# Hybrid mLSTM, dilated attention and MoE block: landing places of the first adaLN weights, the order of the expert matmuls, router and output by halves

## The reference, cut to what matters

```python
mod = silu(c) @ ada_w + ada_b                      # adaLN: 1024 -> 6 * 1024 (sh_a, sc_a, gt_a, sh_f, sc_f, gt_f)
u = rms_norm(x) * (1 + sc_a) + sh_a
proj = u @ w_in                                    # mLSTM q, k, v, o, gates; attention q, k, v; branch gates
y = sigmoid(g_m) * (h_m @ w_branch_m) + sigmoid(g_a) * (h_a @ w_branch_a)
x = x + gt_a * (y @ w_out)
u = rms_norm(x) * (1 + sc_f) + sh_f
scores = sigmoid(u @ router_w)                     # 16 experts, the best group of 4, the best 2 in it
x = x + gt_f * sum_e combine_e * ((silu(u @ w_gate_e) * (u @ w_up_e)) @ w_down_e)
out = rms_norm(x) * final_norm_g
```

## Time and profile before

| | |
|---|---|
| median of 3 runs | 637.62 us (637.15 to 639.16) |
| the profiled execution's own time | 639.07 us |
| its span | 637.3 us |
| PE busy | 593.4 us (93%), 3581 matmul instructions |
| DVE busy | 326.7 us (51%) |
| ACT busy | 225.2 us (35%) |
| DMA | 184.78 MB, mean 290 GB/s over the span |

### The profile page before, as it was taken

How to read it: one execution, slowest core, us unless ns; L and a number is a source line. 1 busy time by engine, 2 the same in 40 slices (tenths; PEclk the granted TensorE clock), 3 DMA queues, 4 the chain that set the end, 5 groups by cost and what they waited for, 6 DMA issues and landing times.

```text
span 637.3 us, 8441 instructions
## 1 busy us (share of the span) xinstructions
PE 593.4 (93%) x3581; PEld 444.7 (70%) x3581; DVE 326.7 (51%) x515; ACT 225.2 (35%) x300; POOL 5.6 (1%) x13
## 2 busy tenths in 40 slices
PE   4697999999999999999999999889999999998783
PEld 4697988999998888999999886533543533533231
DVE  3895986775758977787454655302212112120103
ACT  3424658544454365665552443201111111110103
POOL 3000000000000000000000000000000000000000
PEclk9997999999999999999999997799999999999997
DMA  8996454877767867725699699199999999999981
GB/s 314 358 359 229 143 194 133 283 259 242 255 216 264 319 214 261 258 77 195 198 338 344 219 374 388 48 398 387 401 387 402 386 401 387 401 387 401 387 325 67
DMA packets 86313, 184.78 MB, mean 290 GB/s; under 512 B 5401, under 2 KB 5505, under 8 KB 86273
## 3 DMA queue, kind: packets, MB, share of 16 engines
q1 hardware_dynamic: 83746, 184.06, 79.9%
q10 hardware_dynamic: 2528, 0.16, 0.3%
HBM read 183.16 MB, written 1.05 MB: 289 GB/s over the span
## 4 chain that ended last, share of the span: by engine, by line
PE 85%; DMA 8%; DVE 3%; ACT 1%; issue 1%; SPq 1%; DVEq 0%; ACTq 0%
PE ps L1287 32%; PE ps L1295 15%; PE ps L1495 14%; PE ps L1506 7%; DMA ring<-in_w_down_e_dram 3%; PE ps L1485 2%; DMA ring<-in_w_gate_e_dram 2%; DMA ring<-in_w_up_e_dram 2%; PE ps L1529 2%; DMA raw<-in_ada_w_dram 1%; PE ps L1235 1%; PE ps L1358 1%; PE ps L1382 1%; PE ps L1397 1%; PE ps L1244 1%
## 5 line engine op out<-in xcount | busy, mean ns | idle before, releaser
L1287 PE MATMUL ps<-u_hi,hi 128*128 128x256 f32 x448 | 130.8, 292 | 9.3 <-DVE u_lo L815 9.3
L755 DVE TENSOR_TENSOR lo<-raw,hi 128x2048 fp32r<-128x2048 f32 x52 | 118.7, 2289 | 35.6 <-ACT hi L514 35.3
L1287 PE MATMUL ps<-u_lo,hi 128*128 128x256 f32 x448 | 128.7, 287 | 0.0
L1287 PE MATMUL ps<-u_hi,lo 128*128 128x256 f32 x448 | 128.6, 287 | 0.0
L1495 PE MATMUL ps<-ring,xe_t 128*64 128x512 f32 x512 | 113.8, 594 | 7.9 <-DMA ring<-in_w_up_e_dram 4.4
L514 ACT CAST hi<-raw 128x2048 fp32r<-128x2048 f32 x52 | 98.8, 1907 | 50.0 <-PE ps L1287 24.8
L1287 PEld LDWEIGHTS ps<-u_hi,hi 128*128 128x128 f32 x448 | 88.0, 196 | 9.6 <-DVE u_lo L815 9.5
L1495 PEld LDWEIGHTS ps<-ring,xe_t 128*64 128x64 f32 x512 | 37.1, 137 | 76.0 <-issue 75.7
L1287 PEld LDWEIGHTS ps<-u_lo,hi 128*128 128x128 f32 x448 | 88.0, 197 | 0.1
L1287 PEld LDWEIGHTS ps<-u_hi,lo 128*128 128x128 f32 x448 | 87.9, 196 | 0.0
L1506 PE MATMUL ps<-ring,he_t 128*64 128x512 f32 x256 | 57.1, 596 | 1.5 <-DMA ring<-in_w_down_e_dram 0.8
(11 more groups left out here) (276 smaller groups left out, 797.0 us busy)
## 6 DMA issues: line engine op xcount, KB each, us to landing
raw<-in_w_in_dram SPq DMA_DIRECT2D x42, 1024.0 KB, 5.3
ring<-in_w_gate_e_dram SPq DMA_DIRECT2D x32, 1024.0 KB, 14.6
ring<-in_w_up_e_dram SPq DMA_DIRECT2D x32, 1024.0 KB, 14.2
ring<-in_w_down_e_dram SPq DMA_DIRECT2D x32, 1024.0 KB, 14.6
raw<-in_ada_w_dram SPq DMA_DIRECT2D x24, 1024.0 KB, 5.5
raw<-in_w_branch_m_dram SPq DMA_DIRECT2D x4, 1024.0 KB, 5.5
raw<-in_w_out_dram SPq DMA_DIRECT2D x4, 1024.0 KB, 7.5
raw<-in_w_branch_a_dram SPq DMA_DIRECT2D x2, 1024.0 KB, 6.4
```

The costliest lines, as they stand in the source:

```text
L755: V.tensor_tensor(lo[b % RING][:], src[:], hi[b % RING][:].bitcast(F32), ALU.subtract).then_inc(lo_ready, 1)
L1287: ins = mm(dst, w[:, k, cols], x[:, k0 + k, :], start=(first and c % 2 == 0 and k == 0 and n == 0), stop=(end and k == KB - 1 and n == 2), ...
```

## The change

- The first eight adaLN pieces get landing places of their own (first_ada) and cover two of eight input rows for shift and scale of one half of the channels; SP issues them, and the first four blocks, without waiting for a buffer (only pieces 6 and 7 wait, for x_ss and x_t). Each is two DMAs and two DVE instructions of 1024 elements. PE's share (L1235) is gone. The later sixteen pieces are one row of two 1024-wide outputs each: one DVE instruction of 2048 elements in place of four of 512.
- x is normalised on ACT instead of DVE. PE first turns the small rows, then makes two f32 matmuls of 512 columns whose result is not used, then turns x. ACT splits block 0 ahead of the copies of x_t; DVE splits it ahead of chan. Block 0 runs channel by channel (k outside) and waits for u_lo one 128-channel piece at a time. The column sums for the second half of u are all made in the middle of block 2. The split of the small gate weights moves from block 1 to block 6.
- Ring: the last slot at 120 KB is replaced by one at 176 KB that comes free earlier (after ffn_col), and chunk loads wait for single chunks (chunk_used) instead of pairs.
- Last block: the logits of the first channels are made inside it, and the turn of the second half of tokens 0 to 127 too.
- xg_lo is made after the one-hot matrix, and the gather first makes the high parts of all four banks, then the low parts.
- Expert matmuls: all of expert 0's chunk, then all of expert 1's; each chunk counts up chunk_used, and its DMA is waited for just ahead of it (group_slots is a generator now).
- Output of a pair: rounding and rest in two halves of 512 columns. After the last pair the scatter, the squares' waits, the result and the stores go by halves too (four stores of 256 KB in place of two of 512 KB).

The diff, cut to its core (the code for more than one visit changes alike):

```diff
-STREAM = ([("ada", a) for a in (0, 1, 4, 5)] + [("w", 0), ("w", 1), ("ada", 2), ("ada", 3), ("w", 2)]
-          + [("ada", 6), ("ada", 7), ("w", 3)])
+FIRST = ([("ada", a) for a in range(4)] + [("w", 0), ("w", 1), ("ada", 4), ("ada", 5), ("w", 2), ("ada", 6), ("ada", 7),
+                                           ("w", 3)])
+STREAM = [item for item in FIRST if item[0] == "w"]
 for _s in range(2, NBLK):
...
+        first_ada = [at(f"first_ada{a}", k, [P, 2, 2, NB]) for a, k in enumerate((96, 104, 112, 144, 48, 72, 164, 156))]
...
-            [140, 148, 192, 96, 80, 88] + last_raw[0:2] + [112, 104] + last_raw[2:4]
+            [140, 148, 192, 96, 176, 80, 88] + last_raw[0:2] + [112, 104] + last_raw[2:4]
             + [32 + 8 * ((NBLK - 3) % RING), 56 + 8 * ((NBLK - 3) % RING), 32 + 8 * ((NBLK - 2) % RING),
-               56 + 8 * ((NBLK - 2) % RING), 32 + 8 * ((NBLK - 1) % RING), 56 + 8 * ((NBLK - 1) % RING), 120])]
+               56 + 8 * ((NBLK - 2) % RING), 32 + 8 * ((NBLK - 1) % RING), 56 + 8 * ((NBLK - 1) % RING)])]
...
+            ada_first = A["ada_w"][0].rearrange("(p k) (m n) -> p k m n", k=KT, m=6)
+            for kind, n in FIRST:
+                if kind == "w":
+                    sp.dma_start(raw[n][:], block_source((kind, n))).then_inc(raw_loaded[n], 16)
+                else:
+                    if n == 6:
+                        after(sp, "x_ss")
+                    if n == 7:
+                        after(sp, "x_t")
+                    j, k = n // KB, 2 * (n % KB)
+                    for i in range(2):
+                        sp.dma_start(first_ada[n][:, i], ada_first[:, k + i, 0:2, j * NB:(j + 1) * NB]
+                                     ).then_inc(ada_landed[n], 16)
...
                 if n == 4:
+                    after(sp, "ffn_col")
+                if n == 5:
                     sp.wait_ge(block_done, BLK_IN + 4)
-                if n in (6, 7):
-                    used_up(sp, ("w", NBLK - 10 + n))
-                if n == 8:
+                if n in (7, 8):
+                    used_up(sp, ("w", NBLK - 11 + n))
+                if n == 9:
                     after(sp, "y_f32_1")
-                if n == 9:
+                if n == 10:
                     after(sp, "y_lo1")
-                if n in (10, 11):
-                    used_up(sp, ("w", NBLK - 12 + n))
-                if n in (12, 14, 16):
-                    sp.wait_ge(block_done, NBLK - 8 + n // 2)
+                if n in (11, 12):
+                    used_up(sp, ("w", NBLK - 13 + n))
+                if n in (13, 15, 17):
+                    sp.wait_ge(block_done, NBLK - 2 + (n - 13) // 2)
                 load_chunk(n)
...
-                sp.wait_ge(group_used, (n - RSLOTS) // 2 + 1)
+                sp.wait_ge(chunk_used, n - RSLOTS + 1)
...
-                sp.wait_ge(out_ready, t + 1)
-                sp.dma_start(out[0, t * P:(t + 1) * P, :], result[:, t, :]).then_inc(stored, 16)
-            sp.wait_ge(stored, 16 * TT)
+                for h in range(2):
+                    sp.wait_ge(out_ready, 2 * t + h + 1)
+                    sp.dma_start(out[0, t * P:(t + 1) * P, h * NB:(h + 1) * NB], result[:, t, h * NB:(h + 1) * NB]
+                                 ).then_inc(stored, 16)
+            sp.wait_ge(stored, 32 * TT)
...
+            after(act, "x_rms")
+            for t in range(TT):
+                ins = A_(x_in[:, t, :], x_in[:, t, :], ACT.Copy, scale=st[:, 6 + t:7 + t])
+            event(ins, "x_norm")
...
+            split_hi(0)
             after(act, "x_t")
...
-            split_hi(0)
-            u_split_hi(0)
+            after(act, "x_up", "chan0")
+            for k in range(KB):
+                event(A_(u_hi[:, k, :], x_t[:, k, :], ACT.Identity, scale=chan[:, 2, k:k + 1], bias=chan[:, 0, k:k + 1]),
+                      f"u_hi0_{k}")
...
-                act.wait_ge(y_out, 2 * n + 2)
-                nc.scalar.copy(y_hi_e[:], y_e[:]).then_inc(y_hi_ready, 1)
+                for h in range(2):
+                    act.wait_ge(y_out, 2 * n + 1 + h)
+                    nc.scalar.copy(y_hi_e[:, h * NB:(h + 1) * NB], y_e[:, h * NB:(h + 1) * NB]).then_inc(y_hi_ready, 1)
...
-                act.wait_ge(moe_done, t + 1)
                 for h in range(2):
+                    act.wait_ge(moe_done, 2 * h + t + 1)
...
+                if a < ADA_FIRST:
+                    j = a // KB
+                    dve.wait_ge(ada_landed[a], 32)
+                    dst = acc_a[:, :, j * NB:(j + 1) * NB]
+                    if a % KB:
+                        dve.wait_ge(ada_done, a)
+                    for i in range(2):
+                        kk = 2 * (a % KB) + i
+                        if kk == 0:
+                            step(V.tensor_scalar(dst, first_ada[a][:, i], cs[:, 0:1], None, ALU.mult))
+                            continue
+                        ins = V.scalar_tensor_tensor(out=dst, in0=first_ada[a][:, i], scalar=cs[:, kk:kk + 1], in1=dst,
+                                                     op0=ALU.mult, op1=ALU.add)
+                        if i == 0:
+                            step(ins)
+                    ins.then_inc(ada_done, 1)
+                    return
...
+                if k:
+                    dve.wait_ge(ada_done, a)
+                dst = mod[:, 2 * h:2 * h + 2, :].rearrange("p m n -> p (m n)")
+                V.scalar_tensor_tensor(out=dst, in0=src[:].rearrange("p k n -> p (k n)"), scalar=cs[:, k:k + 1], in1=dst,
+                                       op0=ALU.mult, op1=ALU.add).then_inc(ada_done, 1)
...
+            for a in range(4):
+                ada(a)
+                if a == 0:
+                    after(dve, "vec_t")
+                    event(V.tensor_copy(vec[:], ps[0][:, 0:104]), "vec")
+            split_lo(0)
+            modulate(0, 1)
+            split_first()
+            split_lo(1)
...
             build_onehot(0)
+            for t in range(TT):
+                after(dve, f"xg_hi{t}")
+                V.scalar_tensor_tensor(out=xg_lo[:, t, :], in0=x_res[:, t, :], scalar=st[:, 14 + t:15 + t],
+                                       in1=xg_hi[:, t, :].bitcast(F32), op0=ALU.mult, op1=ALU.subtract).then_inc(xg_split, 1)
...
+            pe.wait_ge(rows_loaded, 80)
+            event(tr(ps[0][:, 0:104], rows[0:104, :], ident[0:104, 0:104]), "vec_t")
             after(pe, "x_norm")
+            for n in range(2):
+                mm(ps[2 + n][:], ident[:], x_in[:, 0, 0:NB], start=True, stop=True)
...
+                if s == 0:
+                    for k in range(KB):
+                        after(pe, f"u_lo0_{k}")
+                        for c in range(4):
+                            dst = ps[banks[c // 2]][:, (c % 2) * T:(c % 2 + 1) * T]
+                            cols = slice(c * P, (c + 1) * P)
+                            for n, (w, x) in enumerate(((w_hi, x_hi), (w_hi, x_lo), (w_lo, x_hi))):
+                                ins = mm(dst, w[:, k, cols], x[:, k, :], start=(c % 2 == 0 and k == 0 and n == 0), stop=False,
+                                         skip_group_check=True)
+                elif channel_major:
...
+                        if s == EARLY - 1 and c == 2:
+                            after(pe, "x_up")
+                            mod_columns(1, 7)
...
+                            if s == NBLK - 1 and t == 1 and k == 1:
+                                after(pe, "x1_1_t0")
+                                for c in range(KB):
+                                    tr_ins = tr(ps[6][:, c * P:(c + 1) * P], x_res[:, 0, NB + c * P:NB + (c + 1) * P], ident[:])
+                                event(tr_ins, "x1_turn1_t0")
                         if s == NBLK - 1 and t == 0:
                             event(ins, "wo_t0")
+                            after(pe, "x1_turned0", "mod3")
+                            logits(0, 0)
+                            logits(1, 0)
...
+            after(pe, "x1_turned1_t0")
+            logits(0, 1)
+            after(pe, "x1_1_t1")
+            for k in range(KB):
+                ins = tr(ps[7][:, k * P:(k + 1) * P], x_res[:, 1, NB + k * P:NB + (k + 1) * P], ident[:])
+            event(ins, "x1_turn1_t1")
+            after(pe, "x1_turned1_t1")
+            event(logits(1, 1), "logits")
...
+                    for part in parts:
+                        x = (xg_hi, xg_lo)[part]
+                        for t in range(TT):
+                            ins = mm(dst, x[:, t, kk * P:(kk + 1) * P], onehot[:, t, 0:cols],
+                                     start=(part == 0 and kk % 2 == 0 and t == 0), stop=(part == 1 and t == TT - 1),
+                                     skip_group_check=True)
+                if parts[-1] == 1:
+                    ins.then_inc(gathered, 1)
...
             def gate_or_up(bank, half, slots, col):

-                for k in range(KB):
-                    kk = KB * half + k
-                    for s in range(2):
```

(57 more changed lines are left out.)

202 lines of the change are left out of this document (69 added, 133 removed).

## The result

The changed kernel takes **651.42 us** in the median of 4 runs (650.41 to 653.27), the kernel before 638.39 us beside it: a ratio of 1.0208, with a 95% interval of 1.0175 to 1.0241. It is 13 us slower, where 628.7 was forecast and 623 to 635 given as the range. The profiled execution took 650.41 us, with a span of 648.7.

A forecast was written before the change was run, and what follows sets the result against it. Expert-phase DMA transfers were taken as the bound, with PE 10 us to spare. Gains 5.6 + 1.9 + 1.4 = 8.9 us from the profiled 639.07 gave 630.2; the median, 1.45 lower, 628.7; range 623 to 635.

The forecast's parts named there:

- the order of the expert matmuls: Expert matmuls, one expert's chunk after the other: PE starts the other half's work past waiting instructions, so 0 us.
- The slower rival: Expert matmuls: column halves run one after the other, 3.0 us a chunk, PE the bound, 738 us; chance 0.20.
- The margin: Expert phase: PE has 10 us to spare, needing 206 us for eight pairs where transfers allow 216.
- The second rival: Expert phase: a chunk alone runs at 0.22 us per instruction, chunk 19 released 1.7 us sooner, 625 us; chance 0.15.
- Front: Kernel start through block 3: first large matmul at 27.05, block 3 at 50.2, 5.6 us gained in all.
- The third rival: Kernel start: small DMA, falling clock or later weights lose 2 to 4 of 5.6 us, 632 to 634; chance 0.12.
- Router and gather: Between router and experts: low parts of x leave DVE's chain ahead of the tables, 2.1 us gained.
- the last block: Last dense block: first logit instructions and one turn move into it, second half's x comes later, 0.2 us lost.
- Tail: After the last pair: output, scatter, squares and stores by halves overlap, 1.4 us gained, between 0.5 and 2.2.

The follow-up runs named there:

- front_only: Changed kernel with expert matmuls alternating call by call again and the gather, logit and tail changes undone; 632.81 us, ratio 0.9916 to the kernel before.
- no_tail: Changed kernel with expert matmuls alternating call by call again and the last output, scatter and stores whole instead of by halves; 631.26 us, ratio 0.9902.

## Why the prediction was wrong

- **The step that failed is the order of the expert matmuls**, priced at "0 us". It took "PE starts work of the other half past one that waits" from the earlier trace rows and let that reach over 7 waiting instructions; it reaches over 3. The other half then starts 4 steps late in each stretch, a chunk costs PE 2.10 us and not 1.76, and the order loses 23.3 us. The text had said that no row shows how far, took the optimistic end as the nearest to eight steps, and kept that end for most of its chance. A look-ahead over one, all that the trace bore out, is no ground for seven.
- **The slower rival (0.20) named the right place and the right point of decision, and the wrong size.** It priced every chunk at 3.0 us, since it charged each handover. Only the start and the end of an unbroken stretch pay: (239.4 - 37.4) / 96 = 2.10 us a chunk. That is over the 1.86 from which it said PE becomes the bound, by 0.24 x 96 = 23 us and not by 110. So the prediction had no case between 639 and 697, where the truth lay.
- **The margin was right.** "PE has 10 us to spare": two pairs took 52.55 us and take 60.49 (from the gate at 460.02 to the one at 520.51), 4.0 more a pair, so 2.0 a stretch. Four steps are 1.7 of it; what the other 0.3 is was not looked into. Eight pairs are 32, and the first gate, which follows no down, is one stretch more, 1.8 (8.94 against 7.09). 33.8 less 10 is 23.8, near the 23.4 measured.
- **The second rival** (chunk 19 released 1.7 us sooner) is refuted: 3.65 us.
- **Front.** First matmul forecast at 27.05, measured 27.02; block 3 at 50.2, measured 49.70, with the clock up, as taken. Gain forecast 5.6, measured 5.3 by front_only (the changed kernel's trace has 6.2 at 179.32). The third rival falls. This part was reasoned from dates of landings and a queue of work per engine, and the two dates held within 0.5 us. One term was off and did no harm: the transfers were to be in by 39, and block 3's weights land at 41.6, where ACT's split starts. ACT is done with it at 43.54, just when DVE's adaLN work ends (43.53), so the late landing costs nothing. That is luck.
- **Router and gather** 2.1 forecast, 2.7 measured; the last block 0.2 lost forecast, between nothing and 1.1 lost measured.
- **Tail** 1.4 forecast, 2.3 in the traces and 3.0 in the medians. The squares come as much sooner as said (1.6 forecast, 1.7 at the last result); the stores then gain 0.5 where 0.2 were taken off, and the scatter's clock was left out. The lower bound's 0.5 for the stores' fixed time stands in no row.
- In sum 8.9 forecast for all but the order, 10.1 measured (0.9842), and with the order 23.3 lost.

The Trainium skill (TensorE: Matmul & The Clock Gate, "Part 3: Packing small matmuls — row/col tiling") says that matmuls start and end in program order. The runs bear out neither that nor the forecast: in the changed kernel the second chunk's first matmul is under way from 399.60 beside the fifth of the first chunk, and three that are earlier in program order start after it. By that rule of the Trainium skill, runs of two calls would take 25 steps, 10.7 us a group (an estimate from the rule and the step of 0.43), against 7.11 measured.

## What to carry to other kernels

When two streams share PE by halves of its columns, alternate them at least every four instructions (two f32 calls); a longer run costs its excess over four in steps, once at each start of such work. This was measured for f32 matmuls of 512 columns and runs of up to eight. Before changing the order of calls within a group, work out what engine would become the bound and at what price: here 0.1 us a chunk was harmless and 0.24 more was 23 us. A full DMA row does not say that DMA is the bound; look at whether it is still full at the end, and at what the last group waited for.

## What was not expected of the hardware

- PE starts work for the free column half past three waiting instructions and not past more (0, 0, 2 and 4 steps of 0.43 us lost for runs of 2, 4, 6 and 8).
- Two f32 matmuls of 512 columns whose result nobody uses, done by 16.5 us, go with a clock of 0.65 to 0.98 from 20 to 24 us in ten traces, against 0.50 in the one without them. They gain no time where PE is not awaited.
- The moment at which the clock falls differs from run to run of like kernels. Behind the same wait of 3.7 us the scatter ran at the lower level from its first matmul in no_tail, and from the fifth on in the kernel before. Where ACT sets the tail this costs nothing; in no_tail it goes with 0.7 us more.
